# Hybrid attention trunk on one core: branch A projected straight into features, GpSimd's conversions in four pieces

## The reference, cut to what matters

```python
def mla_branch(c_q, c_kv, k_rope, q_norm, kv_norm, w_uq, w_ukv, cos, sin):
    q = (rms_norm(c_q, q_norm) @ w_uq).reshape(bsz, seq, A_HEADS, A_NOPE + A_ROPE)      # 192 -> 4 x (64 + 32)
    q_nope = q[..., :A_NOPE]
    q_rope = apply_rope(q[..., A_NOPE:], cos[:, None, :], sin[:, None, :])
    kv = (rms_norm(c_kv, kv_norm) @ w_ukv).reshape(bsz, seq, A_HEADS, A_NOPE + A_V)     # 128 -> 4 x (64 + 64)
    k_nope, v = kv[..., :A_NOPE], kv[..., A_NOPE:]
    k_rope = apply_rope(k_rope, cos, sin)                                               # 32, shared by the heads
    # scores = (q_nope . k_nope + q_rope . k_rope) * (A_NOPE + A_ROPE) ** -0.5, causal softmax, times v

def apply_rope(x, cos, sin):
    x1, x2 = x[..., :half], x[..., half:]
    return jnp.concatenate([x1 * cos - x2 * sin, x1 * sin + x2 * cos], axis=-1)
```

## Time and profile before

| | |
|---|---|
| time, median of 3 runs | 770.52 us (767.0 to 772.05) |
| the profiled execution | 768.9 us, span in the profile 767.0 us |
| TensorE busy | 690.5 us (90% of the span) |
| VectorE, ScalarE, GpSimd busy | 450.4, 328.7, 218.4 us |
| mean granted TensorE clock | 0.954 of full |
| last fill of GpSimd in layer 1 ends, next conversion starts | 270.7, 281.5 us |
| first scores of branch A in layer 1 (L1301) start | 321.0 us |
| output projection of layer 1 starts | 345.8 us |
| a strip of 256 KB, from issue to landing, median | 4.6 us |

### The profile page before, as it was taken

The page is one execution under the profiler, slowest core; times in us unless marked ns, Lnnn a source line. Parts: engine busy times, 40 slices in busy tenths (PEclk is TensorE's granted clock), DMA queues, the critical chain, the costliest instruction groups (busy, mean ns, idle before and its releaser), DMA issues. The chain is left out here.

```text
span 767.0 us, 10353 instructions
## 1 busy us (share of the span) xinstructions
PE 690.5 (90%) x3836; PEld 553.9 (72%) x3836; DVE 450.4 (59%) x1067; ACT 328.7 (43%) x750; POOL 218.4 (28%) x91
## 2 busy tenths in 40 slices
PE   3996999998989899889998999999898989988996
PEld 2885877787776674448997887788787767444896
DVE  4211597987688645561182158888978864556214
ACT  4422534654223445571434345456432344457221
POOL 1332241424035430200335342324323543020020
PEclk9998999997899976999999999999999997699999
DMA  8457963423122110202353487542322221020112
GB/s 259 123 188 233 258 185 111 124 76 106 55 69 69 69 56 1 109 1 80 96 157 111 129 254 228 157 138 69 98 70 68 70 70 56 0 108 3 43 42 110
DMA packets 66753, 81.47 MB, mean 106 GB/s; under 512 B 10720, under 2 KB 52320, under 8 KB 66703
## 3 DMA queue, kind: packets, MB, share of 16 engines
q1 hardware_dynamic: 66703, 80.81, 34.2%
HBM read 70.28 MB, written 13.93 MB: 110 GB/s over the span
## 5 line engine op out<-in xcount | busy, mean ns | idle before, releaser
L694 POOL TENSOR_TENSOR w_low<-w_raw,w_high 128x2048 fp32r<-128x2048 f32 (+2 forms) x39 | 175.8, 4507 | 435.3 <-ACT w_high L733 435.3
L1215 PE MATMUL bank<-uT,w_high 128*128 128x512 f32 x400 | 161.2, 403 | 0.0
L1217 PE MATMUL bank<-uT,w_low 128*128 128x512 f32 x400 | 159.2, 398 | 0.0
L1216 PE MATMUL bank<-uT,w_high 128*128 128x512 f32 x400 | 159.1, 398 | 0.0
L837 ACT ACTIVATE probs<-probs,negmax 128x128 f32<-128x128 f32 (+3 forms) x160 | 89.1, 560 | 99.6 <-DVE negmax L1070 99.0
L1215 PEld LDWEIGHTS bank<-uT,w_high 128*128 128x128 f32 x400 | 76.2, 190 | 18.7 <-issue 1.9
L1217 PEld LDWEIGHTS bank<-uT,w_low 128*128 128x128 f32 x400 | 76.2, 190 | 18.0
L1216 PEld LDWEIGHTS bank<-uT,w_high 128*128 128x128 f32 x400 | 76.3, 191 | 16.5
L733 ACT ACTIVATE w_high<-w_raw 128x2048 fp32r<-128x2048 f32 (+2 forms) x40 | 74.7, 1868 | 29.8 <-DMA w_raw<-in_w_out 23.7
L1215 PE MATMUL bank<-w_high,mix 128*128 128x256 f32 x256 | 72.4, 283 | 1.0 <-DVE mix L1155 1.0
L1216 PE MATMUL bank<-w_low,mix 128*128 128x256 f32 x256 | 71.6, 280 | 0.0
(11 more groups left out here) (145 smaller groups left out, 1119.0 us busy)
## 6 DMA issues: line engine op xcount, KB each, us to landing
w_raw<-in_w_in SPq DMA_DIRECT2D x28, 1024.0 KB, 5.4
w_raw<-in_w_out SPq DMA_DIRECT2D x8, 1024.0 KB, 4.9
parts_dram<-staging SPq DMA_DIRECT2D x12, 512.0 KB, 5.9
strips<-strips_dram SPq DMA_DIRECT2D x24, 256.0 KB, 4.6
dqk<-parts_dram SPq DMA_DIRECT2D x24, 256.0 KB, 4.3
hX<-in_x SPq DMA_DIRECT2D x8, 512.0 KB, 5.8
strips_dram<-table_dram SPq DMA_DIRECT2D x1, 3328.0 KB
qidx<-parts_dram SPq DMA_DIRECT2D x12, 256.0 KB, 4.2
```

Of the source, the lines that this page charges most:

```text
L694: nc.gpsimd.tensor_tensor(w_low[:, s, :, 0:w], w_raw[:, s, :, 0:w], w_high[:, s, :, 0:w].bitcast(F32), ALU.subtract).then_inc(w_low_done, 1)
L1215: nc.tensor.matmul(out_ap, lh, rh, start=start, stop=False)
L1216: nc.tensor.matmul(out_ap, lh, rl, start=False, stop=False)
L1217: return nc.tensor.matmul(out_ap, ll, rh, start=False, stop=stop)
```

## The change

Branch A's steps become other ones. `aq` (one per head) multiplies the head's query weights with the latents of all 512 tokens, so that the bank holds features by tokens: 64 plain features, the 32 rotary ones, and the same 32 with their halves exchanged. ScalarE copies the first 64 rows, VectorE multiplies the other 64 with a table `trig` (cosines above, signed sines below). The keys carry the rotated rotary key twice, so a contraction over 128 features gives the rotary product. The query's own root is no longer applied to queries but as a column, `negroot`, in the shift of A's scores. `aroot` spreads the key latents' roots over all partitions by a matmul with the identity, and VectorE scales `latkv` with it; `ak` (two heads each) and `av` (two token blocks each) then only need copies by ScalarE. GpSimd rotates the key in three products at ("norm", 8), SyncE loads its half-exchanged copy ahead of that and spreads the result to all heads' key rows after it. The weights of A come by eight DMAs instead of three. `low` issues four instructions of two k-slices each.

```diff
-             10: [("aup", 0), ("aup", 1), ("aturn", 0)],
-             11: [("aup", 2), ("aturn", 1), ("aup", 3), ("aturn", 2), ("aturn", 3)]}
+             10: [("aq", 0), ("aq", 1), ("aroot",), ("aq", 2)],
+             11: [("aq", 3), ("ak", 0), ("ak", 1), ("av", 0), ("av", 1)]}
...
+LOW_KS = 2
...
-            cost += {"unit": 1 if s[0] == "unit" and GROUPS[GI[s[1]]][2] else 2, "aup": 1, "pv": 1}.get(s[0], 0)
+            cost += {"unit": 1 if s[0] == "unit" and GROUPS[GI[s[1]]][2] else 2, "aq": 1, "ak": 1, "pv": 1}.get(s[0], 0)
...
                 if step == ("norm", 3):
-                    sp.dma_start(wuq[:, 0, :], mla_w_uq[l, 0:P, :]).then_inc(a_loaded, 16)
-                    sp.dma_start(wuq[0:QL - P, 1, :], mla_w_uq[l, P:QL, :]).then_inc(a_loaded, 16)
-                    sp.dma_start(wukv[:], mla_w_ukv[l]).then_inc(a_loaded, 16)
+                    half = A_ROPE // 2
+                    for c, (first, n) in enumerate(((0, P), (P, QL - P))):
+                        cols = mla_w_uq[l, first:first + n, :].rearrange("p (h d) -> p h d", h=HEADS)
+                        sp.dma_start(wuq[0:n, c, :, 0:A_QK], cols).then_inc(a_loaded, 16)
+                        sp.dma_start(wuq[0:n, c, :, A_QK:A_QK + half], cols[:, :, A_QK - half:A_QK]
+                                     ).then_inc(a_loaded, 16)
+                        sp.dma_start(wuq[0:n, c, :, A_QK + half:P], cols[:, :, HD:HD + half]).then_inc(a_loaded, 16)
...
+                    sp.wait_ge(scores_ready, l * NS + NS_IDX)
+                    sp.dma_start(trig[HD:P, :], rope).then_inc(trig_loaded, 16)
+                if step == ("norm", 8):
+                    sp.wait_ge(bias_ready, (l + 1) * HEADS)
+                    wait_unit_emptied(sp, l * NU + UNIT_AT[("unit", "cq", 1)])
+                    sp.dma_start(trig2[HD:A_QK, :], rope[A_ROPE:2 * A_ROPE, :]).then_inc(krx_loaded, 16)
+                    sp.dma_start(krx[HD:HD + 16, :], latq[HD + 16:A_QK, 1, :]).then_inc(krx_loaded, 16)
+                    sp.dma_start(krx[HD + 16:A_QK, :], latq[HD:HD + 16, 1, :]).then_inc(krx_loaded, 16)
+                if step == ("norm", 9):
+                    sp.wait_ge(kr_ready, l + 1)
+                    sp.wait_ge(scores_ready, l * NS + NS_IDX + S_AT[8])
+                    for first in (HD, A_QK):
+                        sp.dma_start(aqk[first:first + A_ROPE, 1, :, :],
+                                     latq[HD:A_QK, 1, :].unsqueeze(1).to_broadcast([A_ROPE, HEADS, SEQ])
+                                     ).then_inc(krope_loaded, 16)
...
-                nc.gpsimd.tensor_tensor(w_low[:, s, :, 0:w], w_raw[:, s, :, 0:w], w_high[:, s, :, 0:w].bitcast(F32),
-                                        ALU.subtract).then_inc(w_low_done, 1)
+                for k in range(0, KC, LOW_KS):
+                    ks = slice(k, k + LOW_KS)
+                    ins = nc.gpsimd.tensor_tensor(w_low[:, s, ks, 0:w], w_raw[:, s, ks, 0:w],
+                                                  w_high[:, s, ks, 0:w].bitcast(F32), ALU.subtract)
+                ins.then_inc(w_low_done, 1)
...
+                if step == ("norm", 8):
...
+                    raw, turn = latq[HD:A_QK, 1, :], krx[HD:A_QK, :]
+                    nc.gpsimd.tensor_tensor(raw, raw, trig[HD:A_QK, :], ALU.mult).then_inc(kr_step, 1)
+                    pool.wait_ge(kr_step, 2 * l + 1)
+                    nc.gpsimd.tensor_tensor(turn, turn, trig2[HD:A_QK, :], ALU.mult).then_inc(kr_step, 1)
+                    pool.wait_ge(kr_step, 2 * (l + 1))
+                    nc.gpsimd.tensor_tensor(raw, raw, turn, ALU.add).then_inc(kr_ready, 1)
+                    pool.wait_ge(kr_ready, l + 1)
...
+                if kind == "aq":
+                    n = l * NU + UNIT_AT[step]
+                    act.wait_ge(unit_ready, n + 1)
+                    nc.scalar.activation(aqk[0:HD, 0, step[1], :], bank[0:HD, unit_bank(n), :], ACT.Copy
+                                         ).then_inc(high_written, 1)
...
+                        scale = negroot[:, q:q + 1] if br == "A" else -1.0
...
+                if kind == "aroot":
...
+                    nc.vector.tensor_tensor(latkv[:], latkv[:], bank[:, unit_bank(n), :], ALU.mult
+                                            ).then_inc(emptied_by["dve"], 1)
+                if kind == "aq":
...
+                    dve.wait_ge(high_written, highs(n))
+                    nc.vector.tensor_tensor(aqk[HD:P, 0, step[1], :], bank[HD:P, unit_bank(n), :], trig[HD:P, :],
+                                            ALU.mult).then_inc(emptied_by["dve"], 1)
...
-                            ins = nc.tensor.matmul(b, aqk[0:A_QK, 0, h, qs], aqk[0:A_QK, 1, h, ks],
+                            ins = nc.tensor.matmul(b, aqk[:, 0, h, qs], aqk[:, 1, h, ks],
...
+                if kind == "aq":
+                    h = step[1]
+                    pe.wait_ge(a_folded, l + 1)
+                    b = work_bank(l * NU + UNIT_AT[step])
+                    nc.tensor.matmul(b, wuq[:, 0, h, :], latq[:, 0, :], start=True, stop=False)
+                    nc.tensor.matmul(b, wuq[0:QL - P, 1, h, :], latq[0:QL - P, 1, :], start=False, stop=True
+                                     ).then_inc(unit_ready, 1)
```

More of the change, by code:

```diff
@@ L74 @@
 SEL_BLOCKS = (3, 2, 1)
-N_CONSTS = 12
+N_CONSTS = 10
 TOPK_ROUNDS = 3 * TOPK // 8
@@ L241, in units_of @@
         return ["dve"]
-    if k == "aup_head":
-        return ["dve", "dve"]
-    if k == "aup":
-        return ["dve", "act"]
-    if k == "aturn":
-        return ["act", "act"]
+    if k in ("aup_head", "aq", "aroot"):
+        return ["dve"]
+    if k in ("ak", "av"):
+        return ["act"]
     return []
@@ L256, in highs_of @@
         return [units_of(step) == ["dve"]]
+    if step[0] == "aq":
+        return [True]
     return [False] * len(units_of(step))
@@ L391, in trunk @@
         room("wukv", 2 * KB)
-        room("wuq", 3 * KB)
-        room("small", 4 * KB)
+        room("wuq", 4 * KB)
+        room("small", 3 * KB)
         w_raw = at("w_raw", "raw", [P, SLOTS, KC, GW], F32)
@@ new lines, in _ @@
+                    nc.scalar.activation(aqk[0:HD, 0, step[1], :], bank[0:HD, unit_bank(n), :], ACT.Copy
+                                         ).then_inc(high_written, 1)
+                if kind == "ak":
+                    n = l * NU + UNIT_AT[step]
+                    act.wait_ge(unit_ready, n + 1)
+                    for half in range(2):
+                        ins = nc.scalar.activation(aqk[0:HD, 1, 2 * step[1] + half, :],
+                                                   bank[HD * half:HD * (half + 1), unit_bank(n), :], ACT.Copy)
+                    ins.then_inc(emptied_by["act"], 1)
@@ L1399, in _ @@
+                if kind == "av":
+                    b = work_bank(l * NU + UNIT_AT[step])
+                    for half in range(2):
+                        tb = 2 * step[1] + half
+                        ins = nc.tensor.matmul(b[:, half * 256:(half + 1) * 256], latkv[:, tb * P:(tb + 1) * P],
+                                               wukv[:, 1, :], start=True, stop=True)
+                    ins.then_inc(unit_ready, 1)
                 if kind == "ya":
```

153 lines of the change are left out of this document (55 added, 98 removed).

## The result

The changed kernel takes 746.54 us (median of 4 executions, 742.82 to 748.49), the kernel before 771.28 beside it (4 executions, 767.0 to 779.35). The ratio is 0.9684, 95% interval 0.9639 to 0.973: faster by 3.2%. Forecast was 743, range 727 to 760.

The account below looks back on a forecast made before the run. TensorE, busy 90% of the span, was taken to bound the kernel through its work, idle time and clock. Gains of 15.2 (pieces), 9.4 (branch A) and 3.1 us (clock) sum to 27.7, giving 743 us, range 727 to 760.

Parts of the forecast that it names:

- Pieces: GpSimd's low-half conversions in four instructions let VectorE in between: 7.6 us a layer, 15.2 us in all.
- the rival that GpSimd keeps it out: GpSimd's next piece wins the shared port against waiting VectorE, losing the pieces' gain: 762 us, chance 0.08.
- 3.0 at the bv units: At 217, odsq ends 3.5 us earlier, so TensorE's 3.00 us wait for a bank goes: gain 3.0 us a layer.
- 2.1 for the relu waits: At 84 and 96, index accumulations start earlier and TensorE's waits for the relu go: gain 2.1 us a layer.
- 2.5 at 258.8: Two VectorE scalings (L984) finish earlier beside a conversion; TensorE's 2.80 us wait shrinks to 0.3: gain 2.5 us a layer.
- Later conversions at nothing: Conversions end 0.6 us later, within the bq group's 1.1 us cover: cost 0, at most 1 us a layer.
- Branch A on TensorE: Branch A's new steps take 13.2 us a layer at full clock instead of 17.0: gain 3.8 us.
- The scale of A's scores from a column: nothing: VectorE's 32 shifts of A's scores take a column instead of a constant; the engine has room, so cost nothing.
- The clock term: Gain from less half clock, priced at 0.46 us per us of dip; 3.1 us counted for one dip.
- the 265.73 dip: A 6.83 us half-clock dip in each layer after the 2.80 us idle time; one of two counted as gone, 3.1 us.
- the 17 us dip at 282.80: Half-clock stretch beginning in aup_head's one-column sums, which stay; left unchanged, no gain or loss counted.
- slower rival: Clock stays low from the sums at 282.8 to the output projection, 785 us (0.04), or to A's scores, 762 (0.06).

Follow-up runs that it names:

- e1: Kernel before with only GpSimd's low half split into four instructions: 742.56 us, ratio 0.9679 to the kernel before.
- e2: Changed kernel with GpSimd's low half in one instruction again, so branch A's new steps alone: 770.29 us, ratio 0.9852 to the kernel before.
- e6: Changed kernel with each aq's second matmul over 128 input rows, the added weights zero, instead of 64: 736.61 us.
- e9: e1 with the old branch A's second matmul of each query projection over 128 rows (zero weights added) instead of 64: 741.52 us.
- e4: Changed kernel with step aq 2 moved from job 10 to the start of job 11: 748.23 us.
- e10: Changed kernel with constant -1.0 instead of the column as scale in branch A's shifts, leaving the queries' root out of the result: 744.57 us.
- e5: Changed kernel with aup_head's one-column sums made as 64-column matmuls: 747.92 us.
- e8: Kernel before with GpSimd's low half in eight instructions and nothing else: 741.76 us.
- e3: Changed kernel with GpSimd's low half in eight instructions instead of four: 740.30 us.
- e11: Changed kernel with aq's second matmul over 128 rows and the low half in eight instructions, aq 2 left in place: 735.79 us.
- e12: Changed kernel with aq's second matmul over 128 rows and aq 2 moved to job 11, low half in four instructions: 730.93 us.

## Why the prediction was right, and where not

**Pieces: right in size, other in make-up.** 15.2 forecast, 14.5 measured (e1). A waiting VectorE is let in between two pieces; the rival that GpSimd keeps it out is refuted by the rows at 171 and 249. Term by term: 3.0 at the bv units was 3.1 in the table; 2.1 for the relu waits was 2.2; 2.5 at 258.8 was 1.5, since the stage's idle time went from 2.80 not to 0.3 but to 1.3 (22.64 less 21.38 busy, against 25.69 less 22.89): 0.54 remains at this wait and the rest is spread. What I had left out is cqq to ck, 1.6 us a layer. There the same odsq line ran into a conversion in the first differential job too (3.89 us at 174.46), and TensorE waited 1.98 us for what hung on it (L977's result). It was in the trace, below the waits with the largest sums. The four terms make 8.4 a layer, 16.8 in both, 2.3 more than the executions of e1 show at full clock; where these went isn't located. The upper bound of 16.2 is a slip of the sum: 15.2 and twice 0.3 are 15.8.

**Later conversions at nothing, the rotary key, SyncE's DMAs at nothing: right.** No wait on w_low by GpSimd, on krope or on the aq banks above 0.5 us stands in the list of waits. The stretch from the unit before the bq group to its start is 7.31 us before and 7.32 after.

**Branch A on TensorE: right before the clock.** Forecast 3.8 us a layer at full clock; the stage shows 3.0 to 3.4. e2, the pair e6 and e9, and the pair e1 and the changed kernel give 5.4, 5.0 and 6.3 for both layers, that is 2.5 to 3.2 a layer after the price behind it. A part of what is missing is the 2.71 us wait for `turned`: the prediction named the products that queue behind VectorE's new wait and priced them at nothing. e4 shows that this place costs 0.7 (full-clock span) to 0.9 us (idle time) a layer. A second term was too small: "the 64-row half of aq has the same columns, so I give it the same". An aq takes 2.11 us at full clock where the sum had 1.94, 0.7 a layer, and the 0.97 was itself read behind a 64-row matmul; among full rows it is 0.86 (e6). The two together are more than the 0.6 that is missing, so something else in the stage must have come out cheaper, which isn't located.

**"The scale of A's scores from a column: nothing": wrong**, by a small size. VectorE has room on average, not in A's scores, where it stands on TensorE's path. The stage grew by 0.94 us a layer at full clock, of which the column is 0.43 (e10).

**The clock term: near in sum, wrong in both parts.** Counted were 3.1 for the 265.73 dip and 1.8 (twice 0.9) for shorter steps at half clock, 4.9. The medians fell by 24.7 us, of which 20.8 is at full clock, so the clock gave 3.9. But e1 gives what the pieces alone do: 28.7 against the same median (25.3 against the one of its own comparison), 14.5 at full clock, so 11 to 14 from the clock; and branch A on top of that lost 10: 6.3 better at full clock and 4.0 worse in time. Part of what the pieces gave is in the table: in layer 1 the 13.65 us dip at 183.81 is gone, which follows the odsq wait that I had not counted (6.3). For branch A, the step of the prediction that failed is "the 17 us dip at 282.80 begins in the one-column sums, which stay; I leave it": where it begins says nothing of how long it lasts. e5 shows that widening the sums doesn't end it. The prediction's slower rival named this stretch, though not what lengthens it. With aq's second matmul over 128 rows in place of 64 (e6) the stretch halves, and the clock is near that of e8 and e1. Since the steps get shorter by the same edit, and the pair e3 and e11 shows hardly any of it, how the rows act on the clock stays open.

On the page of the Trainium skill that the prediction weighed (TensorE: Matmul & The Clock Gate, "Part 4: PE-mode transpose"): by its rule the stretch would have ended early, with 32 transposes a layer gone. It lasted 20.5 and 23.9 us instead of 17.1, so here that rule didn't decide. Whether transposes count was not tried by itself.

**In sum** 15.2, 7.6 and 4.9 stand against 14.5, 6.3 and 3.9: each a little less, together 3.0 us; the rest of the distance between 743 and 746.5 is the median of the kernel before, 0.8 us higher now than in the runs that the forecast started from. The last of the three agrees by chance, as two things of some 10 us stand against each other in it. The clock between variants of one kernel goes from .945 to .976, some 21 us, as much as the whole change gains at full clock.

**Its signs.** odsq takes 1.69 us on average (said: near 1.6, from 4.4), the wait at the second conversion is 0.54 (under 0.5), no wait stands on the bv units, and past the fourth aq the clock is low only for 3.4 us in layer 1, among A's scores. "Full clock after job 8's scaling" holds in layer 2 only: in layer 1 there are 3.4 us at half clock.

## What to carry to other kernels

Where one engine's long instruction blocks another's short ones, cut it in pieces, and count the gain at every wait that hangs on a blocked one, not at the largest sums alone; an engine with room on average may still set the pace in one stage, so price there what an edit adds to it. Compare variants at equal clock before judging a part: in measured time branch A looked worthless (742.6 us without it, 746.5 with it), at equal clock it is worth 5 to 6 us, and with the rows filled up with zeros in both kernels 4.9 of it shows in the time. A matmul over half of the rows is not free of charge beside full ones: read its price from start to start, not from its duration.

## What the runs showed of the hardware

- A plain f32 matmul over 64 rows costs more time in a row of matmuls over 128 than one over 128 does, though the columns are the same: for 512 columns at full clock, 1.06 us from start to start against 0.86, and its neighbours over 128 rows take about 0.1 more each. For 384 columns, three matmuls of an aup take 2.62 us with the 64-row one in the middle and 2.22 without.
- Kernels with the rows filled ran at a higher granted clock in the new branch A: .963 to .965 against .951 to .958 (e6), .967 to .976 against .945 to .952 (e12 and e4), .962 to .969 against .957 to .965 (e11 and e3). In the old one they didn't: .960 to .972 against .966 to .977 (e9 and e1). What makes the difference is not shown.
- The same list gets different clocks in its two layers: e3 spent 6.8 and 17.1 us of the same stage at half clock, e2 6.8 and 27.3. The granted clock isn't a function of the stage's instructions alone.
- GpSimd's subtractions and VectorE's instructions of the kinds named here take turns by instruction. A conversion of four pieces beside them lasts 5.4 to 6.0 us, alone 5.0 to 5.1; odsq takes 1.56 to 1.82 us beside pieces of 1.3 us and 3.89 to 4.88 beside a whole conversion of 4.6.
- A scale from a column instead of a constant takes 60 ns more in VectorE's shift, at 128 as at 512 elements.
